# Eight-tile projections in one set of PSUM columns, and the first two outputs of a stage chunk by chunk

## The reference, cut to what matters

```python
x = x + mla_mixer(rms_norm(x, g), ...)      # ends with  o @ w_o        (wo_a)
x = x + sqrelu_mlp(rms_norm(x, g), w1, w2)  # up_0, down_0
x = x + mlstm_mixer(rms_norm(x, g), ...)    # ends with  out @ w_o      (wo_m)
x = x + sqrelu_mlp(rms_norm(x, g), w1, w2)  # up_1, down_1
x = x + 0.5 * glu(rms_norm(x, g))           # glu_0, out_0
x = x + conv(rms_norm(x, g))                # cin, cout
x = x + 0.5 * glu(rms_norm(x, g))           # glu_1, out_1
...                                         # keys and values; glu_2, out_2; sparse attention (wo_n); glu_3, out_3
def rms_norm(x, g):
    return x * rsqrt(mean(x * x) + EPS) * g
```

## Time and profile before

| | |
|---|---|
| median of 3 runs | 1744.57 us (1744.33 to 1748.87) |
| the profiled execution | 1747.81 us, its span 1746.0 us |
| mean granted clock of TensorE | 0.972 of 2.4 GHz |
| TensorE matmul, busy | 1638.2 us, 94% of the span |
| VectorE, busy | 1112.7 us, 64% |
| ScalarE, busy | 888.2 us, 51% |
| GpSimd, busy | 182.8 us, 10% |
| weight loads | 522 of 512 KB, 161 GB/s read and written over the span |

### The profile page before, as it was taken

The page is one execution under the profiler, slowest core; times in us unless marked ns, Lnnn a source line. Parts: engine busy times, 40 slices in busy tenths (PEclk is TensorE's granted clock), DMA queues, the critical chain, the costliest instruction groups (busy, mean ns, idle before and its releaser), DMA issues.

```text
span 1746.0 us, 33340 instructions
## 1 busy us (share of the span) xinstructions
PE 1638.2 (94%) x11364; PEld 1526.6 (87%) x11364; DVE 1112.7 (64%) x1794; ACT 888.2 (51%) x1476; POOL 182.8 (10%) x149
## 2 busy tenths in 40 slices
PE   5898999999799999999997999998999988789999
PEld 5687998887699889998996999888999877779998
DVE  5566666635676566666776666776566728676665
ACT  5474554444555444445444544554545547644443
POOL 5550000065100000000000000000000043200000
PEclk9898999999999999999998999999999989999999
DMA  5224555543455565555553555656455680045554
GB/s 205 73 62 144 182 188 185 168 146 132 133 179 181 185 189 177 183 181 193 193 182 131 172 183 184 195 181 212 148 186 185 204 170 20 1 145 181 180 193 144
DMA packets 81708, 282.77 MB, mean 162 GB/s; under 512 B 8800, under 2 KB 13408, under 8 KB 81632
## 3 DMA queue, kind: packets, MB, share of 16 engines
q1 hardware_dynamic: 77840, 276.88, 48.5%
q10 hardware_dynamic: 3792, 4.85, 1.6%
HBM read 280.12 MB, written 1.57 MB: 161 GB/s over the span
## 4 chain that ended last, share of the span: by engine, by line
PE 82%; DVE 7%; ACT 4%; issue 4%; DMA 1%; ACTq 1%; DVEq 1%; POOL 0%; SPq 0%
PE psum L1615 17%; PE psum L1623 15%; PE psum L1624 15%; PE psum L1625 15%; PE psum L1616 9%; PE psum L1734 2%; PE psum L1735 2%; PE psum L1736 2%; ACT xs L521 1%; ACT arena L840 1%; DVE ssq L1046 1%; DVE w_lo L956 1%; DMA raw<-tiles 1%; DVE xs L979 1%; PE psum L1989 1%
## 5 line engine op out<-in xcount | busy, mean ns | idle before, releaser
L507 ACT ACTIVATE w_hi<-raw 128x1024 fp32r<-128x1024 f32 x522 | 550.4, 1056 | 502.3 <-PE psum L1625 310.0
L956 DVE TENSOR_TENSOR w_lo<-raw,w_hi 128x1024 fp32r<-128x1024 f32 x468 | 572.0, 1223 | 237.7 <-ACT w_hi L507 237.3
L1623 PE MATMUL psum<-xs,w_hi 128*128 128x256 f32 x1960 | 564.8, 288 | 48.5 <-DVE xs L979 47.1
L1624 PE MATMUL psum<-xs,w_hi 128*128 128x256 f32 x1960 | 559.9, 286 | 0.0
L1625 PE MATMUL psum<-xs,w_lo 128*128 128x256 f32 x1960 | 559.7, 286 | 0.0
L1615 PE MATMUL psum<-hs,w_hi 128*128 128x512 f32 x1280 | 444.4, 390 | 1.8 <-DVE w_lo L956 1.1
L1623 PEld LDWEIGHTS psum<-xs,w_hi 128*128 128x128 f32 x1960 | 381.8, 195 | 53.7 <-DVE xs L979 39.9
L1624 PEld LDWEIGHTS psum<-xs,w_hi 128*128 128x128 f32 x1960 | 382.0, 195 | 0.5
L1625 PEld LDWEIGHTS psum<-xs,w_lo 128*128 128x128 f32 x1960 | 381.7, 195 | 0.0
L1616 PE MATMUL psum<-hs,w_lo 128*128 128x256 f32 x1280 | 360.9, 282 | 0.0
L1615 PEld LDWEIGHTS psum<-hs,w_hi 128*128 128x128 f32 x1280 | 240.3, 188 | 52.4 <-issue 1.4
(11 more groups left out here) (276 smaller groups left out, 1758.9 us busy)
## 6 DMA issues: line engine op xcount, KB each, us to landing
raw<-tiles SPq DMA_DIRECT2D x522, 512.0 KB, 3.4
bias<-bias_dram ACTq DMA_DIRECT2D x8, 256.0 KB, 13.8
x<-x_in SPq DMA_DIRECT2D x1, 1024.0 KB, 8.4
y_out<-x SPq DMA_DIRECT2D x8, 128.0 KB, 3.1
con<-consts SPq DMA_DIRECT2D x1, 771.0 KB, 9.2
bias_dram<-bias_row ACTq DMA_DIRECT2D x1, 512.0 KB, 7.3
row<-rows SPq DMA_DIRECT2D x1, 192.0 KB, 9.7
vec<-vecs SPq DMA_DIRECT2D x1, 80.5 KB, 3.3
```

Source lines behind the costliest of these rows:

```text
L507: act.activation(w_hi[s][:, :], raw[s][:, :], ACT.Copy).then_inc(hi_ready, 1)
L956: dve.tensor_tensor(w_lo[s][:, :], raw[s][:, :], hi_of(w_hi[s][:, :]), ALU.subtract).then_inc(lo_ready, 1)
L1623: pe.matmul(out, w_hi[s][:, c:c + P], x_hi, start=first, stop=False)
L1624: pe.matmul(out, w_hi[s][:, c:c + P], x_lo, start=False, stop=False)
```

## The change

`residual_one` uses `narrow_product`, and runs its first two outputs chunk by chunk together. `feature` does the same with its first two outputs, where the norm's sums belong to the stage and it has more than one output (`dq` is left out); the sums now stand ahead of the last chunk. VectorE and ScalarE get functions `residual_one` of their own, for `cout` too: the output is added to x in one step, VectorE makes the weight part of the tile before after that add, and ScalarE splits the weight tile after the activation's half and square. The norm's row of the convolution is multiplied into its result chunk by chunk (`conv`), in place of `cout`'s own multiply.

```diff
@@ ScalarE
+            def residual_one(name):
+                t0, o0, gain = TILE0[name], OUT0[name], VEC[NEXT[name]]
+                act.preload_act_table(ACT.Sqrt)
+                with act.Fori(0, KD // 4) as i:
+                    for u in range(4):
+                        xo = at(x, i * (4 * S) + u * S, S)
+                        act.wait_ge(out_read, i * 4 + (o0 + u + 1))
+                        split_x(at(xs, i * (8 * S) + u * 2 * S, S), xo, at(vec, i * 4 + (gain + u), 1))
+                        act.activation(sq[u][:, :], xo, ACT.Square).then_inc(sq_ready, 1)
+                        split(t0 + u + RING, i)
@@ VectorE
+            def residual_one(name):
+                t0, o0, norm_ = TILE0[name], OUT0[name], NEXT[name]
+                if name != "cout":
+                    dve.wait_ge(lo_ready, t0 + RING)
+                for o in range(KD):
+                    xo = x[:, o * S:(o + 1) * S]
+                    dve.wait_ge(tile_done, t0 + o + 1)
+                    dve.tensor_tensor(xo, bank((o0 + o) % 4, 0, S), xo, ALU.add).then_inc(out_read, 1)
+                    if o:
+                        take_lo(t0 + o - 1 + RING)
+                    rest_x(lo_part(xs, o), xo, vec[:, VEC[norm_] + o:VEC[norm_] + o + 1], hi_part(xs, o), XS0[norm_] + o + 1)
+                    dve.wait_ge(sq_ready, SQ0[name] + o + 1)
+                    dve.wait_ge(ssq_ready, SSQ0[norm_] + o + 1)
+                    dve.tensor_tensor(ssq[:, :], ssq[:, :], sq[o % 4][:, :], ALU.add).then_inc(ssq_ready, 1)
+                take_lo(t0 + KD - 1 + RING)
@@ VectorE, conv
+                        then(dve.tensor_tensor(conv_y[j], conv_y[j], rb[:, :], ALU.mult))
                         dve.wait_ge(tile_done, i * 12 + (t0 + 3 * m + 3))
                         dve.tensor_tensor(conv_y[j], b_, conv_y[j], ALU.mult).then_inc(out_read, 1)
@@ TensorE, feature
+                def two():
+                    pe.wait_ge(lo_ready, t0 + 2)
+                    pe.wait_ge(out_read, o0 + 1 - 3)
+                    for k in range(KD):
+                        pe.wait_ge(xs_ready, XS0[xs_name] + k + 1)
+                        if norm_ and k == KD - 1:
+                            sums(norm_)
+                        for u in range(2):
+                            ins = narrow_product((o0 + u) % 4, ((t0 + u) % RING, k * P), k, src, k == 0, k == KD - 1)
+                            if k == KD - 1:
+                                ins.then_inc(tile_done, 1)
...
+                paired = norm_ is not None and outs > 1 and name != "dq"
+                if paired:
+                    two()
+                for u in range(2 if paired else 0, head):
@@ TensorE, residual_one
-                    ins = product((o0 + o) % 4, ((t0 + o) % RING, c * P), c, src, c == 0, c == KD - 1)
+                    ins = narrow_product((o0 + o) % 4, ((t0 + o) % RING, c * P), c, src, c == 0, c == KD - 1)
...
                 for c in range(KD):
                     pe.wait_ge(*ready(c))
                     chunk(0, c)
+                    chunk(1, c)
                     if c in between:
                         between[c]()
-                for o in range(1, KD):
+                for o in range(2, KD):
```

More of the change, by code:

```diff
@@ L240, in build @@
         half0, hid0, sil0, n_half, n_hid, n_sil = {}, {}, {}, 0, 0, 0
-        SCALED = ["down_0", "down_1", "out_0", "cout", "out_1", "out_2", "out_3"]
+        SCALED = ["down_0", "down_1", "out_0", "out_1", "out_2", "out_3"]
         for name, _, outs in STAGES:
@@ L901, in _ @@
             act.dma_start(bias_dram, bias_row[:, :].unsqueeze(1).broadcast_to((H, COPIES, 2 * S))).then_inc(bias_out, 16)
-            residual("wo_a", 1)
+            residual_one("wo_a")
             root("ffn_0")
@@ L906, in _ @@
             mlstm()
-            residual("wo_m", 1)
+            residual_one("wo_m")
             root("ffn_1")
@@ L915, in _ @@
             conv()
-            residual("cout", 1)
+            residual_one("cout")
             root("post_0")
@@ L930, in _ @@
             nsa()
-            residual("wo_n", 1)
+            residual_one("wo_n")
             root("post_1")
@@ L1023, in four @@
                             take_lo(t0 + u * per + j + RING, i * per)
[L1024 to L1036, removed]
+                        dve.wait_ge(half_ready, i * 4 + (h0 + u + 1))
+                        dve.tensor_tensor(f, bank(b, 0, S), half[b][:, :], ALU.add).then_inc(out_read, 1)
+                        dve.wait_ge(out_read, i * 4 + (o0 + u + 1))
+                        dve.tensor_tensor(f, f, rs[:, :], ALU.mult).then_inc(r_scaled, 1)
+                        dve.wait_ge(r_scaled, i * 4 + (x0 + u + 1))
+                        dve.tensor_tensor(xo, f, xo, ALU.add).then_inc(x_ready, 1)
                         if name in NEXT:
@@ L1046, in four @@
                             dve.tensor_tensor(ssq[:, :], ssq[:, :], sq[u][:, :], ALU.add).then_inc(ssq_ready, 1)
-                if name in ("wo_a", "wo_m", "wo_n"):
-                    dve.wait_ge(lo_ready, t0 + RING)
                 if name in NEXT:
@@ L1106, in conv @@
                 with dve.Fori(0, KD // 4) as i:
-                    steps.base, start, steps.n = i * 12 + steps.n, steps.n, 0
+                    steps.base, start, steps.n = i * 16 + steps.n, steps.n, 0
                     for m in range(4):
@@ L1129, in conv @@
                         h_lo(name, conv_y[j], i * (8 * S) + m * 2 * S, i * 4 + (h0 + m + 1))
-                    assert steps.n == 12
-                    steps.base, steps.n = 0, start + 12 * (KD // 4)
+                    assert steps.n == 16
+                    steps.base, steps.n = 0, start + 16 * (KD // 4)
             def out_lo(name, chunks=range(KD), gain=None):
@@ L1670, in feature @@
                         between[u]()
-                    if norm_ and u == norm_at:
+                    if norm_ and not paired and u == norm_at:
                         sums(norm_)
```

24 lines of the change are left out of this document (9 added, 15 removed).

## The result

The changed kernel takes 1694.32 us, median of four runs (1687.26 to 1695.91), against 1746.72 us of the kernel before beside it (1744.33 to 1749.24). The ratio is 0.969, with a 95% interval of 0.967 to 0.9709: faster by 52 us, forecast was 54. The profiled execution takes 1695.91 us, its span 1694.1 us (51.9 us less than before), at a mean granted clock of 0.984 (0.972 before).

What follows compares the result with a forecast made beforehand. TensorE was held up by waits for VectorE's split activations, 47.1 us in 18 waits. Savings at four projections with their next starts, `mgate`, `glu_0` and `cin` summed to 54.1 us, from 1744.57 to 1690.5; range 1680 to 1707.

Steps and rivals of the forecast that it cites:

- VectorE's chain: Four projections: VectorE's work per output falls from 3.77 to 2.32 us, under TensorE's 2.88, leaving no backlog at stage end.
- Weight parts one tile later: Projections: weight parts and slot loads come a tile later, with about 3 us spare for loads; costed at nothing.
- Narrow products: Four projections: 256 products become three matmuls each, from 0.35 to 0.36 us; 0.6 us per stage, 2.6 us in all.
- First two outputs together: Seven stage starts: 14 products cover the wait for the last chunk; 6.10 us to the third tile.
- The small stalls left out: First outputs of `wo_a` and `wo_n`: pairing may hide stalls of 0 to 2 us, not in the sum.
- Convolution: Eight multiplies enter VectorE's loop where it idles 0.66 us for ScalarE; costed at nothing, 4.4 us if uncovered.
- The clock: Stage starts: clock expected at 1.00; rival keeps 0.61 at four projections and `mgate`, costing 11.5 us: 1702, chance 0.09.
- Late weight parts: Rival at seven stage starts: fifth tile's split and weight part exposed, 16 us come back: 1707, chance 0.13.
- VectorE is still the pace: Rival in the projections: VectorE's chain stays above 2.88 us, backlog remains, gain only 29 us: 1716, chance 0.05.
- The weight loads: Rival in narrow products: loads no longer run under matmuls, 0.585 us per product: 1776; slower given chance 0.03.
- the seven places: Four projections with the following stage starts, plus `mgate`, `glu_0` and `cin`: together 54.1 us saved.

Runs made afterwards that it cites:

- order_only: two_sets with the first outputs apart, leaving only the new order on VectorE and ScalarE: 1706.04 us, 0.9756 of the kernel before.
- two_sets: Changed kernel with two column sets and two adds per output in the four projections, new order and paired first outputs kept: 1694.38 us, ratio 0.9696.
- reorder_only: Changed kernel without the pairing of first outputs; new order and one column set kept: 1708.19 us, 0.9784 of the kernel before.
- one_set_only: old_order with the first outputs apart, leaving only the single column set with one add: 1720.14 us, 0.9838 of the kernel before.
- pair_only: Kernel before with only the first two outputs run together; two column sets, two adds and old order stay: 1733.32 us, ratio 0.9913.
- old_order: Changed kernel with the old order of VectorE and ScalarE in the four projections; one column set, one add and pairing kept: 1707.24 us, ratio 0.9765.
- later_still: late_turn with the gate rows and score products one unit later in `mv`, last two numerators two units later in `mo`: 1685.82 us, ratio 0.9646.
- second profile: Profile from running the changed kernel once more with nothing altered: 1694.05 us, 0.9697 of the kernel before.
- late_turn: Changed kernel with the turning of the gate rows and the score products moved later in stage `mv`: 1691.52 us, 0.9672 of the kernel before.

## Why the prediction was right, point by point

**VectorE's chain.** Right. 2.32 us forecast, 2.20 measured, and idle time of 0.53 to 0.55 us ahead of the add once it has caught up. The order alone does it in the three `wo_*`, as order_only and two_sets show; the single set is not needed. The prediction gave one sum for both and could not say that. In `cout` the sum came out as well (14.7 forecast, 15.1 measured), but there the order is the smaller part.

**Weight parts one tile later.** Right at nothing: after the change, TensorE has no wait for `w_lo` in the four projections or at the fifth tile of the next stages, though a load lands in 4.1 us in the first profile instead of 3.4 (in the second it is 3.3).

**Narrow products.** The mis-sized term. In `wo_a` eight of them take 142.61 - 139.77 = 2.84 us, 0.355 each. The 0.36 of the earlier trace rows is the right pace of `up_0`, where 240 narrow products take 86.40 us, before and after; I carried it to another stage. The wide form has no single pace either. In `wo_a` of two_sets eight take 138.71 - 135.89 = 2.82, in `wo_m` of the kernel before 456.50 - 453.73 = 2.77, by these rows of TensorE:

```profile
135.89 0.39 PE L1633 MATMUL psum<-os,w_hi 128*128 128x512 f32 x1
...
138.71 0.39 PE L1633 MATMUL psum<-os,w_hi 128*128 128x512 f32 x1
```

```profile
453.73 0.39 PE L1615 MATMUL psum<-os,w_hi 128*128 128x512 f32 x1
...
456.50 0.39 PE L1615 MATMUL psum<-os,w_hi 128*128 128x512 f32 x1
```

So the narrow form costs 8 x 0.02 = 0.2 us at most in `wo_a` and `wo_n`, 8 x 0.07 = 0.6 in `wo_m`, and 0.4 in `cout` (2.77 to 2.83), in all 1.4 us at most instead of 2.6. Why one form has several paces no run shows. The Trainium skill, "TensorE: Matmul & The Clock Gate", section "Back-to-back issue gap", which I had set aside for the rows, gives 325 and 328 ns, by a formula that it states for a single matmul by itself: its difference of 3 ns lies between the 2 ns of `wo_a` and the 8 ns of `wo_m`, its absolute figures lie some 20 to 30 ns below.

**First two outputs together.** Right: 6.10 us forecast, 6.18 measured in four stages. In `mgate` sums and two products were to take 1.72 us and take 1.67 (332.40 to 334.07). In `glu_0` the sums start 637.64 - 632.38 = 5.26 us behind the first matmul, so 0.22 us of the squares are exposed, not 0.14. That `mgate` gave just the 5.2 us of the forecast is partly luck: without the pair, on the same code and behind the same two waits (1.04 and 0.85 us), it took 12.1 us in the kernel before, 10.6 and 10.5 in reorder_only and order_only, 9.0 in one_set_only, at a granted clock of 0.72, 0.84, 0.84 and 1.00.

**The small stalls left out.** The four projections with their starts gave 0.9, 0.8, 0.4 and 0.9 us more than forecast, 3.0 in all. By the paces above, about half of that is the narrow form's smaller cost. The rest fits the 0 to 2 us of stalls in the first outputs; no experiment separated them.

**Convolution.** Right at nothing. VectorE still idles 0.67 us there for ScalarE, behind the multiply, as it did ahead of it.

**The clock.** Right at the starts: 1.00 instead of 0.61. Cut into slices of 2 us and summed as (1 - granted clock) x length, the kernel before lost 48.0 us, of it 20.4 at the starts of `up_0`, `up_1`, `glu_1`, `glu_3` and in `mgate`; all of these are gone, so the low clock was over a third of the gain. After, 27.5 us are lost. But the premise that the shorter pauses of `glu_0` leave the clock at 1.00 does not hold in every profile: in one_set_only the stage has the same pauses, and from its start to the third tile the clock read 0.83.

**Rivals.** Late weight parts did appear in the variants: 18.8 us in pair_only, 5.2 in old_order, 2.5 in two_sets. "VectorE is still the pace" is nearest to old_order, at 1707 and not 1716. The weight loads stayed hidden: 0.355 us per product, with 190 to 193 ns for a load in the page's groups.

**What the sum lacked.** It took every stage that the change doesn't touch as unchanged. In the first profile they gave back 4.7 us net, against 2.6 that the seven places gave more than forecast: the span fell by 51.9 us instead of 54.1. That the sum came so near is also luck, since two errors of opposite sign met in it. The rest of the way from 1690 to 1694 is the kernel before, whose median was 1744.57 at the forecast and 1746.72 beside the result. The 3.2 us in `mv` and `mo` are low clock behind a wait of the same length, shown by the windows, and by later_still, where it went with the wait; whether the change brings them is open, as said. In `glu_2` busy time rose by 1.1 us and the wait for the normalised keys inside it by 0.7. The second profile has neither (busy 136.9 us against 137.1 before, the wait 7.1 against 7.2), so that loss, like the other two differences, lies between two profiles and is not shown to come from the change.

## What to carry to other kernels

Where one engine feeds another per tile, compare their periods: an edit to the feeder pays down to the consumer's period and is worth nothing measurable beyond, so where one edit gets there, a second on the same chain is not needed (0.9756 for the order, 0.9784 with the single set as well). Moving an operation into another operation's pause can do more than removing one (3.77 to 2.66 us, against 3.08). A wait of TensorE is to be priced with the granted clock behind it: 3.46 us of wait in an untouched stage cost an estimated 8.4. And a loss of a few microseconds in a stage that an edit doesn't touch is to be sought in a second profile before it is explained.

## What the runs showed of the hardware

The same wait is not followed by the same low clock. Behind 3.46 us in `mv` the granted clock read 0.64 for 4.7 us before, but 0.50 and 0.58 for 10.8 in the changed kernel and 0.50 and 0.62 for 11.0 in its second profile. Behind 1.04 and 0.85 us in `mgate` it was anything from 0.72 to 1.00 over the stage. About the 2.09 us ahead of the second numerator it read 0.81 over 9 us in late_turn, where it had been 1.00 for 20 us, and stayed at 1.00 in later_still, where it had been 1.00 for 36 at least. That makes a few microseconds between profiles of the same instructions. It does not account for the runs of the changed kernel (1687 to 1697 us in the nine of both series): the quickest of them, 1687.26 us, has a mean granted clock of 0.983, and 1695.91 us has 0.984. What separates them was not measured.
